# Casts of the weight slabs moved forward in ScalarE's queue, and one of its waits moved eight slabs back, in a three-layer kernel on one core

## The reference, cut to what matters

```python
# second layer
a = jnp.exp(log_a)                                   # 1280 channels, gates from sigmoids
norm = jnp.sqrt(-jnp.expm1(2.0 * log_a))
_, h = lax.associative_scan(combine, (a, norm * (i * x)), axis=1)
ya = h * jax.nn.gelu(g_rnn)
yb = spatial_gating(jax.nn.gelu(u), jax.nn.gelu(v), ...)
x = x + (sigmoid(gate_a) * (ya @ w_branch_a) + sigmoid(gate_b) * (yb @ w_branch_b)) @ w_out
...
# third layer, mixer_block
h_m = head_rmsnorm(sigmoid(mo) * mlstm(mq, mk, mv, li, lf), g_hm)      # mLSTM
lg  = log_sigmoid(llr @ w_gla_lr + b_gla) / GLA_TAU
h_l = head_rmsnorm(gla(lq, lk, lv, lg), g_hl) * silu(lr)               # gated linear attention
h_d = head_rmsnorm(gated_deltanet(gq, gk, gv, g_dec, beta), g_hd) * silu(dz)
up  = einsum('bsnc,ncd->bsnd', stack([h_m, h_l, h_d]), w_up)
return sum(sigmoid(gates) * up, axis=2) @ w_out
```

## Time and profile before

| | |
|---|---|
| median of three runs | 3088.87 us (3088.44 to 3089.86) |
| profiled execution | 3085.53 us |
| its span, first to last instruction | 3083.7 us |
| TensorE busy | 2916.3 us (95%) |
| VectorE, ScalarE, GpSimd busy | 1262.2, 1149.0, 1496.0 us |
| mean granted TensorE clock | 0.977 |

### The profile page before, as it was taken

The page is one execution under the profiler, slowest core; times in us unless marked ns, Lnnn a source line. Parts: engine busy times, 40 slices in busy tenths (PEclk is TensorE's granted clock), DMA queues, the critical chain, the costliest instruction groups (busy, mean ns, idle before and its releaser), DMA issues.

```text
span 3083.7 us, 41172 instructions
## 1 busy us (share of the span) xinstructions
PE 2916.3 (95%) x15600; PEld 2298.2 (75%) x15600; DVE 1262.2 (41%) x2023; ACT 1149.0 (37%) x1678; POOL 1496.0 (49%) x1883
## 2 busy tenths in 40 slices
PE   7999969899999998999999999989998887999998
PEld 6777648788888885867888887757777676888886
DVE  4066474554211645142362225151475633562222
ACT  4534533443222427234342224243544424442222
POOL 5445502256555674536565554515226324665553
PEclk9999989999999999999999999989999899999999
DMA  4323200233333332325322222312112103422222
GB/s 138 103 90 93 66 1 3 88 118 97 99 93 96 134 104 86 109 69 195 124 95 96 96 96 89 122 45 89 65 59 84 53 26 134 169 94 96 96 96 82
DMA packets 80673, 284.16 MB, mean 92 GB/s; under 512 B 8968, under 2 KB 9096, under 8 KB 79744
## 3 DMA queue, kind: packets, MB, share of 16 engines
q1 hardware_dynamic: 66240, 236.36, 23.3%
q10 hardware_dynamic: 13296, 41.97, 3.6%
q0 software_dynamic: 976, 3.56, 0.4%
HBM read 260.86 MB, written 20.99 MB: 91 GB/s over the span
## 4 chain that ended last, share of the span: by engine, by line
PE 41%; issue 27%; POOL 25%; DVE 3%; ACT 2%; DMA 0%; POOLq 0%; ACTq 0%; SPq 0%; DVEq 0%
POOL slab_r L2988 25%; PE bank L366 11%; PE bank L368 10%; PE bank L367 10%; PE bank L615 2%; PE bank L592 1%; PE bank L686 1%; PE bank L734 1%; PE bank L499 1%; PE bank L509 1%; PE bank L991 0%; PE bank L673 0%; PE bank L1096 0%; PE bank L795 0%; ACT slab_high L1241 0%
## 5 line engine op out<-in xcount | busy, mean ns | idle before, releaser
L2988 POOL TENSOR_TENSOR slab_r<-slab,slab_high 128x256 fp32r<-128x256 f32 x1768 | 1397.0, 822 | 1352.9 <-ACT slab_high L1241 1346.1
L366 PE MATMUL bank<-xh,slab_high 128*128 128x512 f32 x2256 | 909.0, 403 | 31.8 <-POOL slab_r L2988 26.6
L368 PE MATMUL bank<-xh,slab_r 128*128 128x512 f32 x2256 | 884.7, 392 | 0.0
L367 PE MATMUL bank<-x_raw_r,slab_high 128*128 128x512 f32 x2064 | 810.4, 393 | 0.0
L1241 ACT CAST slab_high<-slab 128x1024 fp32r<-128x1024 f32 x442 | 462.1, 1046 | 450.0 <-DMA slab<-in_w_down 216.4
L367 PE MATMUL bank<-work_r,slab_high 128*128 128x512 f32 x1376 | 543.0, 395 | 0.0
L366 PEld LDWEIGHTS bank<-xh,slab_high 128*128 128x128 f32 x2256 | 428.0, 190 | 151.3 <-POOL slab_r L2988 32.4
L368 PEld LDWEIGHTS bank<-xh,slab_r 128*128 128x128 f32 x2256 | 427.5, 189 | 93.0
L366 PE MATMUL bank<-work_r,slab_high 128*128 128x512 f32 x1184 | 469.2, 396 | 23.5 <-DMA cst<-in_cst 15.9
L368 PE MATMUL bank<-work_r,slab_r 128*128 128x512 f32 x1184 | 471.5, 398 | 0.0
L367 PEld LDWEIGHTS bank<-x_raw_r,slab_high 128*128 128x128 f32 x2064 | 391.9, 190 | 81.1 <-issue 3.3
(11 more groups left out here) (463 smaller groups left out, 2714.5 us busy)
## 6 DMA issues: line engine op xcount, KB each, us to landing
slab<-in_w_down SPq DMA_DIRECT2D x88, 512.0 KB, 3.5
slab<-in_w_up SPq DMA_DIRECT2D x64, 512.0 KB, 3.5
slab<-in_w_gates SPq DMA_DIRECT2D x56, 512.0 KB, 3.5
slab<-in_w_merge SPq DMA_DIRECT2D x48, 512.0 KB, 4.1
slab<-in_w_gu SPq DMA_DIRECT2D x44, 512.0 KB, 3.5
slab<-in_w_in_a SPq DMA_DIRECT2D x32, 512.0 KB, 3.5
gates<-staging ACTq DMA_DIRECT2D x56, 256.0 KB, 3.9
slab<-in_w_out SPq DMA_DIRECT2D x24, 512.0 KB, 3.5
```

The source lines that it names most:

```text
L366: first = pe.matmul(bank[b][:, :], wh, mh, start=start, stop=False)
L367: pe.matmul(bank[b][:, :], wh, ml, start=False, stop=False)
L368: end = pe.matmul(bank[b][:, :], wl, mh, start=False, stop=stop)
L2988: low = pool.tensor_tensor(slab_low[:, slot, at], slab[:, slot, at], plain(slab_high[:, slot, at]), ALU.subtract)
```

## The change

Two new helpers stand for the old `high_next`. `high_ahead` casts the next slab at once and remembers it. `high_turn` stands wherever a cast stood (`send_gate`, the merges, the loops); if a cast was already made ahead, it makes none and takes one off the count. So the order of the casts and their number (442) stay.

```diff
+            ahead = [0]
+            def high_turn():
+                if ahead[0]:
+                    ahead[0] -= 1
+                    return
+                if to_split[0] < total_slabs:
+                    high_part(to_split[0])
+                to_split[0] += 1
+            def high_ahead():
+                high_part(to_split[0])
+                to_split[0] += 1
+                ahead[0] += 1
...
                 elif block_no == 2:
+                    high_ahead()
                     gates_back(block_no, sg, x_from)
                 else:
+                    high_ahead()
                     act.wait_ge(S("branches_ready"), n.next(S("branches_ready")))
...
                 act.activation(W(41 + c), W(41 + c), ACT.Sqrt).then_inc(S("lru_norm"), n.up(S("lru_norm")))
+                if c in (2, 6):
+                    high_ahead()
...
                     floor_copy(h + 1)
+                if h == 1:
+                    high_ahead()
...
             act.activation(W(18, 4), W(18, 4), ACT.Exp, scale=-1.0).then_inc(chain, n.up(chain))
+            high_ahead()
             act.wait_ge(chain, n.own(chain))
             act.activation(W(18, 4), W(18, 4), ACT.Ln, bias=eps["one"]).then_inc(S("lf_parts"), n.up(S("lf_parts")))
+            high_ahead()
...
             act.activation(W(37, 4), W(37, 4), ACT.Ln, bias=eps[1e-06], scale=1.0 / P).then_inc(chain, n.up(chain))
+            high_ahead()
             act.wait_ge(chain, n.own(chain))
             act.activation(W(37, 4), W(37, 4), ACT.Exp, scale=-0.5).then_inc(S("h_rstd"), n.up(S("h_rstd")))
-            act.wait_ge(S("h_used"), n.next(S("h_used")))
-            copy_tiles("in_d", FIRST_D, W3(0, FIRST_D))
+            d0 = tiles("in_d")
+            for t in range(FIRST_D):
+                high_turn()
+                if t == DC:
+                    act.wait_ge(S("h_used"), n.next(S("h_used")))
+                act.wait_ge(psum_for["act"], d0 + t + 1)
+                act.copy(W(t), bank[t % RING][:, :]).then_inc(evac, 1)
...
             for c in range(4):
                 act.activation(W(43 + 2 * c), W(4 + c), ACT.Square).then_inc(S("y_square"), n.up(S("y_square")))
+            high_ahead()
             for c in range(4):
                 act.wait_ge(psum_for["act"], n.next(psum_for["act"]))
                 act.activation(W(c), bank[4 + c % 2][:, :], ACT.Ln, bias=eps[1e-06], scale=1.0 / P)\
                     .then_inc(evac, n.up(evac))
                 act.wait_ge(evac, n.own(evac))
+            high_ahead()
```

More of the change, by code:

```diff
@@ L1241, in high_part @@
                 act.copy(slab_high[:, slot, :], slab[:, slot, :]).then_inc(S("slab_high"), 1)
+            ahead = [0]
[10 more added lines that the diff above has]
+                ahead[0] += 1
             def steps_of(stage, n_slabs, body=None, peel=False):
+                assert not ahead[0], stage
                 s0 = to_split[0]
@@ L1273, in send_gate @@
                 s = t % STAGING
-                high_part(to_split[0])
-                to_split[0] += 1
+                high_turn()
                 act.wait_ge(S("gate_done"), t + 1)
@@ L1310, in copy_tiles @@
                 act.wait_ge(evac, base + total)
[L1312 to L1316, removed]
             def x_tile(stage, c, sem, value):
@@ L1339, in last_of @@
                 for c in range(DC):
-                    high_next()
+                    high_turn()
                     x_tile(following, c, evac_by["dve"], base + c + 1)
@@ L1977, in _ @@
             act.activation(W(37, 4), W(37, 4), ACT.Ln, bias=eps[1e-06], scale=1.0 / P).then_inc(chain, n.up(chain))
+            high_ahead()
             act.wait_ge(chain, n.own(chain))
             act.activation(W(37, 4), W(37, 4), ACT.Exp, scale=-0.5).then_inc(S("h_rstd"), n.up(S("h_rstd")))
-            act.wait_ge(S("h_used"), n.next(S("h_used")))
-            copy_tiles("in_d", FIRST_D, W3(0, FIRST_D))
+            d0 = tiles("in_d")
+            for t in range(FIRST_D):
+                high_turn()
+                if t == DC:
+                    act.wait_ge(S("h_used"), n.next(S("h_used")))
+                act.wait_ge(psum_for["act"], d0 + t + 1)
+                act.copy(W(t), bank[t % RING][:, :]).then_inc(evac, 1)
+            n.seen[psum_for["act"].name] = d0 + FIRST_D
+            n.made[evac.name] = d0 + FIRST_D
+            act.wait_ge(evac, d0 + FIRST_D)
             act.wait_ge(S("conv3_keys"), n.next(S("conv3_keys")))
```

## The result

| | before | after |
|---|---|---|
| median of five runs | 3088.87 us (3087.44 to 3094.47) | 3071.05 us (3070.57 to 3077.22) |
| profiled execution, its span | 3085.53, 3083.7 us | 3070.57, 3068.8 us |
| mean granted TensorE clock | 0.977 | 0.975 |

The ratio is 0.9943, with a 95% interval of 0.9928 to 0.9957: 17.8 us faster, where 16.9 were predicted. The two profiled executions differ by 15.0 us.

What follows compares the result with a forecast made beforehand. TensorE is busy 2916.3 of 3083.7 us; 32.0 us of its waits end with GpSimd's low part, late through ScalarE's casts. Terms 8.8 + 4.3 + 2.3 + 2.0 + 1.5 - 2.0 = 16.9 us give 3072.0 us, range 3065.5 to 3081.

Steps and rivals of the forecast that it cites:

- C: mLSTM, slab 302 cast before the third head's Abs: scores start earlier, 2.3 us won, bounds 0 and 3.8.
- D: Start of the linear attention, slabs 321 and 322 cast earlier: 2.0 us won, bounds 0.6 and 2.2.
- F: DeltaNet's end (slabs 352, 353) and third merge (356), cast earlier: 4.3 us won, bounds 1.3 and 6.3.
- E: Behind the linear attention, slab 329 cast between Ln and Exp, `h_used` wait moved: 8.8 us won, bounds 6.85 to 8.8.
- rival 2: E's wait comes back eight slabs on, at `h_used` or the convolution: 8.1 us won, 3080.8 us; chance 0.07.
- A: LRU, slabs 158 and 159 cast amid square roots: wait moves to slab 163, 2.0 us lost, bounds 0 and -4.0.
- B: Second merge, slab 186 cast where ScalarE only waited for a store: 1.5 us won, bounds 0 and 1.5.
- rival 5: Slower: the casts sit on ScalarE's path in C, D, E and F and are paid: 3096.1 us; chance 0.04.
- Rival 1: Waits only change places in F, C and D as in A: 8.3 us won, 3080.6 us; chance 0.15.
- Rival 4: Slab 322's four subtractions hold VectorE up over its scans, 3.3 us; D gives 0.6: 3073.4 us; chance 0.13.

Runs made afterwards that it cites:

- experiment 2: Changed kernel with slab 163 cast before ScalarE's wait for `ya_ready` (three casts there, not two): 3069.22 us, 0.9939 of the kernel before.
- experiment 1: Changed kernel with the casts of slabs 158 and 159 put back behind the LRU's square roots: 3073.02 us, 0.9943 of the kernel before.
- experiment 8: Changed kernel with the wait for `h_used` at its old place, slab 329 still cast ahead: 3076.68 us, 0.9960 of the kernel before.

## Why the prediction was right, by its own steps

The sum was 16.9 us and the time came 0.9 below it. That is closer than its terms were, and in part luck: C missed by 3.7 us and D by 0.8 the one way, F by 2.0 the other, and the two profiled executions differ by 15.0 us where the medians differ by 17.8.

- **E** was right in full: 8.8 predicted, 9.0 measured, halved stretch included; rival 2 has nothing for it in any run.
- **A** was right in mechanism and size (-2.0; -1.8 and -2.2 in two profiles). The step was "nothing is won, and the halved stretch comes behind 163". It goes on where the prediction stopped: the wait was not VectorE's alone. Of the 6.1 us, 2.7 were ScalarE's cast and GpSimd's low part standing behind `ya_ready` for no reason of data. The halved stretch agrees with the Trainium skill, TensorE: Matmul & The Clock Gate, section What's actually happening: it follows the idle time, whoever ends it.
- **B** was right (1.5; 1.8).
- **C** was wrong in sign. The step that failed was "the scores can start at 2075.73 + 0.69 + 1.04 = 2077.5 instead of 2079.75. So 2.3 us". The start came as computed, 2078.31 with 0.96 of offset. But the prediction priced no clock behind the wait that was left, 2.79 us. Before, the halved clock fell on slab 302's first matmuls and had risen when the sums began; now it fell on the sums, 7.3 us for 4.35, and with it slabs 306 to 320 took another 1.6, in a longer halved stretch there; that the one brings the other isn't shown, only that they come together: in the six profiles whose sums took 7.3 us or more, and in none of the others. Its bounds, 0 to 3.8, hold neither the -3.1 nor the -1.4 of slabs 301 to 306. The size isn't fixed: where the halved clock lasted less, C cost 0.4, and where none fell, it won 1.8, near the forecast 2.3. For C rival 5 has the sign but not the reason: the cast did sit on ScalarE's path, yet the scores began 2.4 us sooner, and what was lost was the clock's. Rival 1, the waits only change places, holds for A and C and not for D and F.
- **D** was right in direction and too small: 2.7 to 2.9 for 2.0, over its bound of 2.2; in the two profiles side by side C's 1.6 us hides that. Mis-sized was ScalarE's part, "they win only where ScalarE stood still: 1.60 us before its third copy": from that copy to the levels it won 1.8 us, not 1.4, as both casts came out of the stretch behind slab 320's transposes, and they were covered by TensorE in front of it. VectorE's part was right (0.64, 0.6 forecast). Rival 4 is refuted: VectorE lost 1.45 us over its scans, against a cover of 1.9. The rule of SBUF — State Buffer in the Trainium skill, section Who interferes with whom, would have VectorE or GpSimd stand still entirely; the trace doesn't agree. In the LRU's 25.45 us of the earlier trace rows GpSimd did twenty subtractions, 14.1 us of work at the 0.70 they take alone, and VectorE 6.7 channels at 3.8, 17.4 us at the 2.6 that one takes alone; that is 31.5 us of work in 25.45. Four subtractions delayed VectorE by 1.45 and 1.6 us, not by 2.8.
- **F** gave 6.3 where 4.3 were forecast, and 4.3 in the mean over eleven profiles. By parts in the profile: slabs 352 and 353 gave 6.3 of standing and clock, as forecast; from TensorE's last wait of 3.42 us in line 499 to slab 351 it is 4.9 us in the three kernels without F and 5.8 in seven of the profiles with it, so the cast in front of the Ln cost 0.9 (1.04 forecast). In the merge 1.0 was to be lost; instead 0.8 was won in the changed kernel: slab 356's 1.8, less a wait for VectorE longer by 1.1, as the gates' transfers landed 0.9 us sooner in the chain and no halved stretch followed. In six other kernels one did, of 0.9 to 1.6 us.

What stays open: the medians fell by 17.8 to 18.8 us in the two sets of runs, while the terms as measured alone (-1.8, 1.8, -3.1, 2.8, 9.0, 4.3) sum to 13.0. With C at +1.8, as where no halved clock fell, it would be 17.9, but no run shows how often that is. The difference is of the size by which halved stretches elsewhere come and go between profiles, and one profile of before doesn't tell whether they come more often there.

## What to carry to other kernels

When work is moved ahead to end a wait, write down the next thing the waiting engine needs and who delays that; put the moved instruction where its own engine stands idle for at least its length, not merely where it is early. Price the clock behind the new wait as well as behind the old one, by what runs there. And a wait on data that the next instruction in the queue doesn't need is worth moving by itself: it was 2.9 us of E, and at slab 163, where the cast was put in front of the wait, 2.7.

## What the runs showed of the hardware

- In front of the third head's scores TensorE's granted clock stayed at 1.00 (2.4 GHz) behind waits of 1.57 to 1.60 us in three kernels, and was at 0.50 (1.2 GHz) for a part of the matmuls behind one of 2.79 to 2.83 us at the same place, in all seven profiles that had it. In the changed kernel line 991's matmuls took 7.3 us then, not 4.35; in experiment 2 some 5.7.
- Behind the same wait the clock doesn't always fall. At slab 286, slab 152 and slab 358 the same code ran a halved stretch in some profiles and none in others, worth 0.9 to 2.9 us each. Nor does the length of the wait tell by itself: behind 1.79 us at slab 286 the clock was halved (experiment 1), behind 2.55 us at slab 330 it stayed at 1.00 (experiment 8). Differences of 2 us between single profiles mean nothing unless they are read at the place of the edit.
- GpSimd's subtraction and VectorE's scans and products slow each other: 1.27 us for 0.70, and 3.8 us for 2.6 per channel of the LRU.
